# Pairs of feed-forward tiles by block products in stage 1, and 62 modulation steps moved into layer 2

## The chip, the cores and the metric

One core of a Trainium2 chip runs the whole kernel in one launch. The metric is the device time in microseconds (us) of that core, and every time below comes from the chip: from the runs of the kernel before or from one profiled execution of it.

## The reference, cut to what matters

Two hybrid layers (retention, gated linear attention, forgetting attention, then a feed-forward stage) are followed by a second block with two more feed-forward stages, all in float32, for 512 positions and a model width of 1024. What the change touches is the modulation and the feed-forward stage of the two hybrid layers:

```python
def hybrid_layer(x, c_act, ...):                     # called for layer 1, then layer 2
    mod = c_act @ w_ada + b_ada                      # 1024 x 6144, one row of c
    shift1, scale1, gate1, shift2, scale2, gate2 = jnp.split(mod, 6, axis=-1)
    h = modulate(rms_norm(x, norm1_g), shift1, scale1)
    ...                                              # three mixers, out projection
    h2 = modulate(rms_norm(x, norm2_g), shift2, scale2)
    u, g = jnp.split(h2 @ w_up, 2, axis=-1)          # 1024 x 5632
    u = causal_dwconv(u, w_conv, b_conv)             # three taps along the positions
    y = (jax.nn.silu(u) * g) @ w_down                # 2816 x 1024
    return x + (gate2[:, None, :] * y).astype(x.dtype)
```

## The kernel before, in words

**Products.** Activations lie transposed in SBUF, a feature per partition and 512 positions per row. Each float32 product is made of three matmuls on rounded parts (hi x hi, hi x lo, lo x hi; L515 to L517 in `dot`). A tile is 128 outputs: 8 blocks of 128 inputs, three matmuls of 512 columns each. A feed-forward stage has 22 columns f, each with an up tile and a gate tile, and two sweeps of 8 down tiles `d` (after f = 7 and f = 14, 7 blocks of inputs each), with a last sweep of 8 behind f = 21 as `out_proj`. The stages are `ffn(0)` and `ffn(1)` in the two hybrid layers and `ffn(2)`, `ffn(3)` in the second block.

**Pairs.** For an f in `PAIRS_OF[i]` the up and the gate tile are made together by a scheme of seven block products rather than eight (`pair` L1259, on PE `half_product` L1253 to L1255: twelve matmuls of 256 columns each). It needs sums of the weight's blocks (DVE `pair_sums`, L3108, L3111, L3113), their rounded parts (ACT `pair_high`, L2083 and following; DVE `pair_low`, L3122, L3127, L3131, where L3127 is the low part of the pair's second chunk), sums and differences of the activations' halves made once a stage (`halves_whole`, `halves_sum`, `halves_low`, L3046 to L3095, and `halves_high` on ACT), and DVE additions into the results (`pair_out`, L3141, L3146, L3150). The sixth of the seven products adds into a bank that ACT copies first (`pair_copies`, L2102: MP). In ACT's program that copy stands behind `pair_high` of the next pair, and so behind the next pair's sums on DVE. `PAIRS_OF` is empty for stage 0 and holds 10, 14 and 14 columns for the others.

**Behind the tiles.** For each f the DVE makes two convolution taps of the up tile (L3019, L3022), multiplies with the gate tile (L3030) and makes the low part FL (L3036); ACT makes silu and FH. `down_update` adds a down tile to X.

**Weights.** They stream through a ring of six slots (`raw`, `hi`, `lo`; NSLOT = 6), one chunk (512 KB, or 448 KB for a down tile) in each. SP issues the loads in order (L3548 here). The load of chunk n waits until chunk n-6 has been used: by the last matmul of its tile or pair (semaphore `dense_product`), or by DVE where the chunk was a modulation chunk (`dve_norm`). ACT rounds the chunk to hi (L1530), POOL makes lo (L3522) for all but the second chunk of a pair.

**Modulation.** `mod` of a layer is 12 row groups q of 512 outputs, each with four chunks of w_ada (`ada`, L2576). A chunk costs two steps of the generator. In the first DVE does two multiply-adds into AA (L2590 for the very first, L2593), with the fourth chunk also a transpose (L2616) and a reduction (L2620). So a layer has 96 steps and 48 chunks. After some of the q (`ADA_LAST`) PE folds the sums over the partitions, 8 records of 4 matmuls (L801), and DVE adds the result into MOD (L2508). These stand in each engine's program where `schedule` puts them: `beside(main, ada, n)` advances the modulation by one step at each of the first n yields of the main work, `weave(main, fill)` at each, and neither does it at a yield of BUSY. Each engine walks the same schedule, so the order is fixed for all.

**What runs where.** Layer 1's own modulation is made in layer 1 (`beside` with 6, 14, 8 and 22 steps), with its last 14 steps at the head of `ffn(0)`; then all 96 steps of layer 2 run in `ffn(0)` and the `out_proj` behind it. Layer 2 has no modulation work of its own.

Of the kernel before, what the change touches and what calls it, by code (L numbers as in the profile page):

```python
# [33 lines left out]
BUSY = "busy"  # L34
# [8 lines left out]

PAIRS_OF = ((),
# [8 lines left out]
DOWN = {7: (0, 7), 14: (7, 7)}  # L53
LAST = 14


# [73 lines left out]

ADA_LAST = ((6, 9, 11), (3, 7, 11))

# [285 lines left out]
def schedule(P):  # L418

    P.startup()  # L420
    P.prologue()
    P.half_left = False
    for l in range(DEPTH):
        P.layer_begins(l)
        P.order = BIG4
        ada = (y for q in range(4, 12) for y in P.ada(0, q)) if l == 0 else iter(())
        drain(beside(P.ret_inputs(l), ada, 6))
# [16 lines left out]

        def fill_next(l=l, ada=ada):
            yield from ada
            if l + 1 < DEPTH:
                for q in range(12):
                    yield from P.ada(l + 1, q)

# [33 lines left out]
class TensorSteps(Steps):  # L484
# [814 lines left out]
    def down(self, i, wd, k0, kn):  # L1299

        m, t = self.m, self.t
        for d in range(KD):
            key = ("down", i, k0, d)
# [4 lines left out]
                      m.vtake.at("ff", i, k0 + k)) for k in range(kn)]  # L1308
            yield from self.dot(self.bank[b][:, :], terms, [key, ("chunk", n)], (m.lo.at(n), self.free[b]))
            self.free[b] = m.vtake.at(*key)  # L1310
# [202 lines left out]
class ScalarSteps(Steps):  # L1513
# [603 lines left out]
    def ffn(self, i):  # L2117

        def take(j):
            self.ffn_jobs(i, j)  # L2120
            if PAIRS_OF[i] and PAIRS_OF[i][0] < 7 and j == 3:
                self.halves_high(i)
            if PAIRS_OF[i] and PAIRS_OF[i][0] >= 7 and 5 <= j <= 8:
                self.halves_high(i, (j - 5,))
# [3 lines left out]
        for f in range(HEAD, KF):  # L2128
# [22 lines left out]
            if f in DOWN:  # L2151
# [6 lines left out]
                for d in range(KD):  # L2158
                    if g is not None and d >= KD - 2:
                        for part in ((0, 1) if d == KD - 2 else (2,)):  # L2160
                            self.pair_high(i, g, part)
                    yield from self.tile()

# [186 lines left out]
class VectorSteps(Steps):  # L2350
# [704 lines left out]
    def halves_sum(self, i, j):  # L3055
# [12 lines left out]
        else:  # L3068
            q.wait_ge(m.vtake.at("whole", i, 3), m.vtake.at("traw", i, 2))
            e.tensor_tensor(R4, R4, R2, ALU.add).then_inc(*m.vtake.up(("traw", i, 3)))  # L3070

    def halves_step(self, i, j):

        spread = PAIRS_OF[i][0] >= 7
        if spread and 1 <= j <= 4:
# [93 lines left out]
    def ffn(self, i):  # L3169
# [9 lines left out]
        for f in range(HEAD, KF):  # L3179
# [16 lines left out]
            if f in DOWN:  # L3196
# [3 lines left out]
                for d in range(KD):  # L3200
# [3 lines left out]
                    if g is not None and d == KD - 1:  # L3204
                        self.pair_low(i, g, 1)
                        self.pair_low(i, g, 2)
                    yield from self.tile()
                    self.down_update(i, DOWN[f][0], d, gate)
        self.late_tile(i, late, None)

# [597 lines left out]
```

## Time and profile before

| | |
|---|---|
| median of 3 runs | 2869.91 us (2868.97 to 2870.55) |
| profiled execution, its own time | 2871.7 us |
| span of that execution | 2869.9 us |
| TensorE busy | 2830.1 us (99%) |
| VectorE busy | 1744.3 us (61%) |
| ScalarE busy | 1217.9 us (42%) |
| GpSimd busy | 1096.6 us (38%) |
| granted TensorE clock, mean | 0.998 |

TensorE is busy for nearly the whole span, so what counts is how long it works and where it waits. The other engines run beside it with room on average; the room differs from stage to stage. The profiled execution lasted 1.8 us longer than the median, and the span is 1.8 us shorter than that execution's own time.

### The profile page before, as it was taken

To read this page: it belongs to the slowest core of one execution; us is meant where nothing else is said; L and a number is where in the kernel's file an instruction comes from. 1 tells how busy PE (TensorE), PEld (TensorE's weight loads), DVE (VectorE), ACT (ScalarE), POOL (GpSimd) and SP (SyncE) were. 2 spreads that over 40 slices of the span, in tenths; PEclk is the share of its full clock that TensorE was granted. 3 is DMA by queue.
4 is the path that set the end of the run, shared out by engine and by line. 5 is a ranking of instruction groups with operands and counts; after the bars stand their busy time and mean duration, and the time that the engine had idled before them with its cause. 6 is when DMAs were issued, how large, how long until landed. Compare 5 with 4: busy or idle time off the path is not lost.

```text
span 2869.9 us, 38579 instructions
## 1 busy us (share of the span) xinstructions
PE 2830.1 (99%) x16103; PEld 2414.1 (84%) x16103; DVE 1744.3 (61%) x2394; ACT 1217.9 (42%) x1861; POOL 1096.6 (38%) x447
## 2 busy tenths in 40 slices
PE   8999999999999999999999999999999999999999
PEld 5777889888888887789898998889999877789998
DVE  5444598667664624437765855648667556576683
ACT  4335344442333424533443434344334466443433
POOL 1332243444445332342444344543334433333432
PEclk9999999999999999999999999999999999999999
DMA  8431344446564422233333333333333322233332
GB/s 259 126 103 52 96 141 131 118 147 204 188 202 125 117 76 59 74 96 96 89 107 94 100 96 94 104 96 90 109 103 103 96 66 69 75 91 98 110 102 75
DMA packets 507297, 314.32 MB, mean 110 GB/s; under 512 B 14290, under 2 KB 478836, under 8 KB 506868
## 3 DMA queue, kind: packets, MB, share of 16 engines
q1 hardware_dynamic: 507124, 311.87, 37.0%
q8 instruction: 127, 2.08, 0.3%
q14 instruction: 46, 0.38, 0.0%
HBM read 309.73 MB, written 2.10 MB: 109 GB/s over the span
## 4 chain that ended last, share of the span: by engine, by line
PE 92%; DVE 4%; ACT 1%; DMA 1%; SPq 1%; POOL 1%; issue 1%; DVEq 0%; ACTq 0%
PE b L515 14%; PE b L517 14%; PE b L516 14%; PE s L516 3%; PE s L515 3%; PE s L517 3%; PE b L1253 3%; PE o L515 3%; PE b L1255 3%; PE b L1254 3%; PE o L516 3%; PE o L517 3%; PE s L1253 2%; PE s L1255 2%; PE s L1254 2%; PE b L1191 1%
## 5 line engine op out<-in xcount | busy, mean ns | idle before, releaser
L3522 POOL TENSOR_TENSOR lo<-raw,hi 128x1024 fp32r<-128x1024 f32 (+3 forms) x437 | 1094.3, 2514 | 1744.1 <-ACT hi L1530 1258.2
L1530 ACT ACTIVATE hi<-raw 128x1024 fp32r<-128x1024 f32 (+1 forms) x440 | 449.6, 1034 | 300.7 <-DMA raw<-in_w_up_dram 93.3
L515 PE MATMUL b<-HH,hi 128*128 128x512 f32 x1080 | 433.4, 401 | 1.6 <-DVE X L2419 1.6
L517 PE MATMUL b<-HH,lo 128*128 128x512 f32 x1080 | 421.2, 390 | 0.0
L516 PE MATMUL b<-HL,hi 128*128 128x512 f32 x1080 | 421.1, 390 | 0.0
L515 PEld LDWEIGHTS b<-HH,hi 128*128 128x128 f32 x1080 | 202.8, 188 | 51.7 <-issue 7.1
L517 PEld LDWEIGHTS b<-HH,lo 128*128 128x128 f32 x1080 | 202.7, 188 | 43.5
L516 PEld LDWEIGHTS b<-HL,hi 128*128 128x128 f32 x1080 | 203.0, 188 | 41.7 <-issue 1.4
L515 PE MATMUL b<-FH,hi 128*128 128x512 f32 (+1 forms) x391 | 144.8, 370 | 1.5 <-POOL lo L3522 1.5
L516 PE MATMUL b<-FL,hi 128*128 128x512 f32 (+1 forms) x391 | 144.5, 370 | 0.0
L517 PE MATMUL b<-FH,lo 128*128 128x512 f32 (+1 forms) x391 | 144.5, 369 | 0.0
L2593 DVE SCALAR_TENSOR_TENSOR AA<-raw,CA,AA 128x512 f32<-128x512 f32 x140 | 139.0, 993 | 3.0
L3036 DVE TENSOR_TENSOR FL<-CB,FH 128x512 fp32r<-128x512 f32 x88 | 84.9, 964 | 64.8 <-ACT FH L2058 64.8
L2083 ACT ACTIVATE EH<-ER 128x1024 fp32r<-128x1024 f32 x38 | 40.3, 1061 | 181.5 <-DVE ER L3108 181.5
L3127 DVE TENSOR_TENSOR lo<-raw,hi 128x1024 fp32r<-128x1024 f32 x52 | 109.2, 2100 | 0.0
L2051 ACT ACTIVATE CB<-CB 128x512 f32<-128x512 f32 x88 | 55.4, 630 | 122.3 <-DVE CB L3022 72.0
L2058 ACT ACTIVATE FH<-CB 128x512 fp32r<-128x512 f32 x88 | 55.6, 631 | 119.4 <-DVE CB L3030 118.3
L515 PE MATMUL s<-HH,hi 128*128 128x512 f32 x232 | 90.3, 389 | 0.0
L516 PE MATMUL s<-HL,hi 128*128 128x512 f32 x232 | 90.3, 389 | 0.0
L517 PE MATMUL s<-HH,lo 128*128 128x512 f32 x232 | 90.2, 389 | 0.0
L515 PEld LDWEIGHTS b<-FH,hi 128*128 128x128 f32 x391 | 73.7, 189 | 14.3 <-POOL lo L3522 1.9
L517 PEld LDWEIGHTS b<-FH,lo 128*128 128x128 f32 x391 | 73.7, 189 | 12.5
(765 smaller groups left out, 7485.6 us busy)
## 6 DMA issues: line engine op xcount, KB each, us to landing
raw<-in_w_up_dram SPq DMA_DIRECT2D x88, 512.0 KB, 4.1
raw<-in_w_ada_dram SPq DMA_DIRECT2D x80, 512.0 KB, 4.9
raw<-in_w_in_dram SPq DMA_DIRECT2D x76, 512.0 KB, 4.0
raw<-in_w_mg_dram SPq DMA_DIRECT2D x48, 512.0 KB, 3.8
raw<-in_ffn_w_gate_dram SPq DMA_DIRECT2D x44, 512.0 KB, 3.8
raw<-in_ffn_w_up_dram SPq DMA_DIRECT2D x44, 512.0 KB, 3.9
raw<-in_w_down_dram SPq DMA_DIRECT2D x32, 448.0 KB, 3.8
raw<-in_ffn_w_down_dram SPq DMA_DIRECT2D x32, 448.0 KB, 4.1
```

The lines of the kernel that those rows point to most:

```text
L515: e.matmul(out, wh, xh, start=start and k == 0, stop=False)
L516: e.matmul(out, wh, xl, start=False, stop=False)
L517: mm = e.matmul(out, wl, xh, start=False, stop=stop and k == last)
L1253: e.matmul(out, wh[:, c], xh[:, k, :], start=start and k == 0, stop=False, skip_group_check=True)
L1254: e.matmul(out, wh[:, c], xl[:, k, :], start=False, stop=False, skip_group_check=True)
L1255: mm = e.matmul(out, wl[:, c], xh[:, k, :], start=False, stop=k == 3, skip_group_check=True)
L1530: e.activation(t["hi"][:, c % NSLOT, 0:w], K.raw[:, c % NSLOT, 0:w], ACT.Copy).then_inc(*m.hi.up(c))
L2058: e.activation(t["FH"][:, f % ROOM, :], t["CB"][:, f % 2, :], ACT.Copy).then_inc(*m.atake.up(("fh", i, f)))
L2593: a = e.scalar_tensor_tensor(out=AA[:, :], in0=raw[:, k * 512:k * 512 + 512], scalar=CA[:, kk:kk + 1], in1=AA[:, :], op0=ALU.mult, op1=ALU ...
L3036: e.tensor_tensor(t["FL"][:, f % ROOM, :], t["CB"][:, f % 2, :], t["FH"][:, f % ROOM, :].bitcast(F32), ALU.subtract).then_inc(*m.vtake.up( ...
L3127: e.tensor_tensor(t["lo"][:, s, :], K.raw[:, s, :], t["hi"][:, s, :].bitcast(F32), ALU.subtract).then_inc(*m.vtake.up(("lo", na + 1 if K.p ...
L3522: e.tensor_tensor(t["lo"][:, s, 0:w], K.raw[:, s, 0:w], t["hi"][:, s, 0:w].bitcast(F32), ALU.subtract).then_inc(*m.lo.up(n))
```

## The change

`PAIRS_OF[0]` becomes (8, 9, 10, 12, 13, 15, 16, 17, 19, 20): ten columns of `ffn(0)` are made as pairs, and f = 4 to 7, 11, 14, 18 and 21 stay direct. The halves of the activations that pairs need are made beside the first down sweep (`halves_beside_down`, ACT's `halves_high` at d = 2 and 3), where no modulation step is taken any more (`rows_beside`). `pair` itself yields BUSY as before, so a pair takes no step either. Layer 2's 96 steps are now one generator `rows` that goes on across the layers: up to 34 of them in `ffn(0)`, behind layer 1's last 14 (48 in all), then 6 + 14 + 8 + 22 = 50 in layer 2's own stages, and the last 12 at the head of `ffn(1)`. `ADA_LAST[1]` gets a fourth fold: (3, 6, 9, 11).

```diff
--- before.py
+++ after.py
@@ -1,5 +1,5 @@
 from contextlib import ExitStack
-from itertools import chain
+from itertools import chain, islice
 
 import concourse.bass as bass
 import numpy as np
@@ -41,7 +41,7 @@
 
 
 
-PAIRS_OF = ((),
+PAIRS_OF = ((8, 9, 10, 12, 13, 15, 16, 17, 19, 20),
             (7, 8, 9, 11, 12, 14, 15, 16, 18, 19),
             (5, 6, 7, 8, 9, 10, 12, 13, 14, 15, 16, 17, 19, 20),
             (5, 6, 7, 8, 9, 10, 12, 13, 14, 15, 16, 17, 19, 20),
@@ -52,6 +52,9 @@
 ROOM = 8
 DOWN = {7: (0, 7), 14: (7, 7)}
 LAST = 14
+def rows_beside(i, f, d):
+    return i > 0 or (f == LAST and d < 7)
+
 
 
 def ffn_next(i, f):
@@ -128,7 +131,7 @@
 
 
 
-ADA_LAST = ((6, 9, 11), (3, 7, 11))
+ADA_LAST = ((6, 9, 11), (3, 6, 9, 11))
 
 
 def ada_group(l, q_):
@@ -420,10 +423,11 @@
     P.startup()
     P.prologue()
     P.half_left = False
+    rows = (y for q in range(12) for y in P.ada(1, q))
     for l in range(DEPTH):
         P.layer_begins(l)
         P.order = BIG4
-        ada = (y for q in range(4, 12) for y in P.ada(0, q)) if l == 0 else iter(())
+        ada = (y for q in range(4, 12) for y in P.ada(0, q)) if l == 0 else rows
         drain(beside(P.ret_inputs(l), ada, 6))
         drain(P.ret_values(l))
         P.order = ["b0", "b1"]
@@ -442,11 +446,10 @@
         P.mods(l, 1)
         drain(P.out_proj("w_o", l, P.x_norm(2 * l + 1)))
 
-        def fill_next(l=l, ada=ada):
+        def fill_next(l=l, ada=ada, rows=rows):
             yield from ada
             if l + 1 < DEPTH:
-                for q in range(12):
-                    yield from P.ada(l + 1, q)
+                yield from islice(rows, 34)
 
         fill = fill_next()
         weave(P.ffn(l), fill, False)
@@ -1306,7 +1309,8 @@
             hi, lo = self.K.slot(n, kn, 128)
             terms = [(hi[:, k, :], lo[:, k, :], t["FH"][:, (k0 + k) % ROOM, :], t["FL"][:, (k0 + k) % ROOM, :],
                       m.vtake.at("ff", i, k0 + k)) for k in range(kn)]
-            yield from self.dot(self.bank[b][:, :], terms, [key, ("chunk", n)], (m.lo.at(n), self.free[b]))
+            for _ in self.dot(self.bank[b][:, :], terms, [key, ("chunk", n)], (m.lo.at(n), self.free[b])):
+                yield None if rows_beside(i, k0 + kn, d) else BUSY
             self.free[b] = m.vtake.at(*key)
 
 
@@ -2118,9 +2122,9 @@
 
         def take(j):
             self.ffn_jobs(i, j)
-            if PAIRS_OF[i] and PAIRS_OF[i][0] < 7 and j == 3:
+            if i > 1 and j == 3:
                 self.halves_high(i)
-            if PAIRS_OF[i] and PAIRS_OF[i][0] >= 7 and 5 <= j <= 8:
+            if i == 1 and 5 <= j <= 8:
                 self.halves_high(i, (j - 5,))
 
         yield from self.projects(range(2 * HEAD), ffn_norm(i), take)
@@ -2159,7 +2163,10 @@
                     if g is not None and d >= KD - 2:
                         for part in ((0, 1) if d == KD - 2 else (2,)):
                             self.pair_high(i, g, part)
-                    yield from self.tile()
+                    for _ in self.tile():
+                        yield None if rows_beside(i, f, d) else BUSY
+                    if i == 0 and f == 7 and d in (2, 3):
+                        self.halves_high(i, (2 * d - 4, 2 * d - 3))
 
 
 
@@ -3069,9 +3076,21 @@
             q.wait_ge(m.vtake.at("whole", i, 3), m.vtake.at("traw", i, 2))
             e.tensor_tensor(R4, R4, R2, ALU.add).then_inc(*m.vtake.up(("traw", i, 3)))
 
+    def halves_beside_down(self, i, d):
+
+        if d < 2:
+            self.halves_whole(i, (2 * d, 2 * d + 1))
+        elif d < 4:
+            self.halves_sum(i, 2 * d - 4)
+            self.halves_sum(i, 2 * d - 3)
+        elif d < 6:
+            self.halves_low(i, (2 * d - 8, 2 * d - 7))
+
     def halves_step(self, i, j):
 
-        spread = PAIRS_OF[i][0] >= 7
+        spread = i == 1
+        if i == 0:
+            return
         if spread and 1 <= j <= 4:
             self.halves_whole(i, (j - 1,))
         elif spread and 5 <= j <= 8:
@@ -3204,8 +3223,11 @@
                     if g is not None and d == KD - 1:
                         self.pair_low(i, g, 1)
                         self.pair_low(i, g, 2)
-                    yield from self.tile()
+                    for _ in self.tile():
+                        yield None if rows_beside(i, f, d) else BUSY
                     self.down_update(i, DOWN[f][0], d, gate)
+                    if i == 0 and f == 7:
+                        self.halves_beside_down(i, d)
         self.late_tile(i, late, None)
 
     def down_update(self, i, k0, d, gate):
```

On SP, the loads behind the first down sweep of `ffn(0)`. Before, every tile's chunk is followed by a modulation chunk, here at the end of the sweep:

```order
152 L3548 DMA raw<-in_w_down_dram 128x7x128 [waits dense_product]
153 L3548 DMA raw<-in_w_ada_dram 128x2x512 [waits dve_norm]
154 L3548 DMA raw<-in_w_up_dram 128x8x128 [waits dense_product]
155 L3548 DMA raw<-in_w_ada_dram 128x2x512 [waits dve_norm]
156 L3548 DMA raw<-in_w_up_dram 128x8x128 [waits dense_product]
```

Now the seven w_up chunks at the top end with 11's up tile; a w_ada chunk, 11's gate tile and another w_ada chunk follow, and then both chunks of pair 12, those of pair 13, and the two tiles of f = 14 with the down sweep:

```order
145 L3570 DMA raw<-in_w_up_dram 128x8x128 [waits dense_product] x7
146 L3570 DMA raw<-in_w_ada_dram 128x2x512
147 L3570 DMA raw<-in_w_up_dram 128x8x128 [waits dense_product]
148 L3570 DMA raw<-in_w_ada_dram 128x2x512
149 L3570 DMA raw<-in_w_up_dram 128x8x128 [waits dense_product]
150 L3570 DMA raw<-in_w_up_dram 128x8x128
151 L3570 DMA raw<-in_w_up_dram 128x8x128 [waits dense_product]
152 L3570 DMA raw<-in_w_up_dram 128x8x128 [waits dve_norm]
153 L3570 DMA raw<-in_w_up_dram 128x8x128 [waits dense_product]
154 L3570 DMA raw<-in_w_ada_dram 128x2x512 [waits dve_norm]
```

What moved: between the chunks of pair 10 and those of pair 12 there are now four others, two direct tiles and two modulation chunks, so that the slots that pair 12's chunks go into are pair 10's. The same holds at f = 18 for pairs 17 and 19.

On DVE, around f = 18 of `ffn(0)`. Before, with modulation steps between direct tiles only:

```order
604 L3036 TENSOR_TENSOR FL<-CB,FH 128x512
605 L2593 SCALAR_TENSOR_TENSOR AA<-raw,CA,AA 128x512 x2
606 L3019 SCALAR_TENSOR_TENSOR CB<-b,PAR,CB 128x511
607 L3022 SCALAR_TENSOR_TENSOR CB<-b,PAR,CB 128x510
608 L2593 SCALAR_TENSOR_TENSOR AA<-raw,CA,AA 128x512 x2
609 L2616 STREAM_TRANSPOSE raw<-AA 128x512
610 L2620 TENSOR_REDUCE AS<-raw 128x16
611 L3030 TENSOR_TENSOR CB<-CB,b 128x512
612 L3036 TENSOR_TENSOR FL<-CB,FH 128x512
```

Now, behind the low parts of pair 19's sums (L3150), the two multiply-adds, transpose and reduction of a row group's last chunk, then the convolution of f = 18:

```order
651 L3150 TENSOR_TENSOR EL<-ER,EH 128x512
652 L2600 SCALAR_TENSOR_TENSOR AA<-raw,CA,AA 128x512 x2
653 L2623 STREAM_TRANSPOSE raw<-AA 128x512
654 L2627 TENSOR_REDUCE AS<-raw 128x16
655 L3026 SCALAR_TENSOR_TENSOR CB<-o,PAR,CB 128x511
656 L3029 SCALAR_TENSOR_TENSOR CB<-o,PAR,CB 128x510
657 L2597 TENSOR_SCALAR AA<-raw,CA 128x512
658 L2600 SCALAR_TENSOR_TENSOR AA<-raw,CA,AA 128x512
659 L2515 TENSOR_TENSOR MOD<-s,PAR 128x16
660 L3037 TENSOR_TENSOR CB<-CB,s 128x512
661 L3043 TENSOR_TENSOR FL<-CB,FH 128x512
662 L3127 TENSOR_TENSOR ER<-raw 128x1024
```

What moved: the reduction (L2627) that the fold on PE waits for stands behind pair 19's sums and low parts, and pair 20's sums (L3127) behind all of it.

On DVE, at f = 5 of `ffn(1)`. Before, only the low parts of the halves (L3095) stand between the tiles' rows:

```order
1074 L3030 TENSOR_TENSOR CB<-CB,b 128x512
1075 L3036 TENSOR_TENSOR FL<-CB,FH 128x512
1076 L3095 TENSOR_TENSOR TL<-TR,TH 128x1024
1077 L3019 SCALAR_TENSOR_TENSOR CB<-o,PAR,CB 128x511
1078 L3022 SCALAR_TENSOR_TENSOR CB<-o,PAR,CB 128x510
1079 L3095 TENSOR_TENSOR TL<-TR,TH 128x1024
1080 L3030 TENSOR_TENSOR CB<-CB,s 128x512
```

Now layer 2's last modulation chunks stand between them as well, with the fold's result added into MOD (L2515):

```order
1171 L3043 TENSOR_TENSOR FL<-CB,FH 128x512
1172 L3114 TENSOR_TENSOR TL<-TR,TH 128x1024
1173 L2600 SCALAR_TENSOR_TENSOR AA<-raw,CA,AA 128x512 x2
1174 L2623 STREAM_TRANSPOSE raw<-AA 128x512
1175 L2627 TENSOR_REDUCE AS<-raw 128x16
1176 L3026 SCALAR_TENSOR_TENSOR CB<-b,PAR,CB 128x511
1177 L3029 SCALAR_TENSOR_TENSOR CB<-b,PAR,CB 128x510
1178 L3114 TENSOR_TENSOR TL<-TR,TH 128x1024
1179 L2515 TENSOR_TENSOR MOD<-o,PAR 128x8
```

What moved: two multiply-adds, a transpose and a reduction have come between FL (L3043) and the next convolution (L3026). On PE the fold of these sums stands in the middle of 5's gate tile.

## Rows read from the trace of the kernel before

**Rows 1.** The page: the chain that ended last, by engine.

```profile
PE 92%; DVE 4%; ACT 1%; DMA 1%; SPq 1%; POOL 1%; issue 1%; DVEq 0%; ACTq 0%
```

**Rows 2.** Timeline of PE, `ffn(2)`: start, duration, operation, [idle before, releaser].

```profile
2044.16 0.28 PE L1253 MATMUL b<-HH,hi 128*128 128x256 f32 x1
...
2074.39 0.40 PE L515 MATMUL s<-HH,hi 128*128 128x512 f32 x1
...
2085.30 0.28 PE L1253 MATMUL b<-HH,hi 128*128 128x256 f32 x1
```

**Rows 3.** Waits of PE, window 908 to 914: total, times, longest, in us.

```profile
PE b L515 <- POOL lo L3522: 1.5, 1, 1.5
```

**Rows 4.** Timeline of PE around a fold, at the end of `ffn(0)`.

```profile
916.80 0.39 PE L517 MATMUL b<-FH,lo 128*128 128x512 f32 x1
...
917.31 0.39 PE L515 MATMUL o<-FH,hi 128*128 128x256 f32 x1
```

**Rows 5.** DMA view, window 2054 to 2062: KB, us from issue to landing.

```profile
raw<-in_ffn_w_gate_dram SPq DMA_DIRECT2D x1, 512.0 KB, 4.0
raw<-in_ffn_w_up_dram SPq DMA_DIRECT2D x1, 512.0 KB, 5.3
```

**Rows 6.** Timeline of DVE in `ffn(1)`, between two groups of pairs.

```profile
1610.69 1.21 DVE L3108 TENSOR_TENSOR ER<-raw 128x1024 f32<-128x1024 f32 x1
...
1616.92 1.21 DVE L3127 TENSOR_TENSOR lo<-raw,hi 128x1024 fp32r<-128x1024 f32 x1
...
1620.04 0.68 DVE L3131 TENSOR_TENSOR EL<-ER,EH 128x512 fp32r<-128x512 f32 x1
1621.05 0.75 DVE L3019 SCALAR_TENSOR_TENSOR CB<-b,PAR,CB 128x511 f32<-128x511 f32 x1 [0.32 <-ACT CB L2044]
...
1623.35 0.69 DVE L3030 TENSOR_TENSOR CB<-CB,b 128x512 f32<-128x512 f32 x1 [0.77 <-ACT CB L2051]
...
1625.34 1.22 DVE L3108 TENSOR_TENSOR ER<-raw 128x1024 f32<-128x1024 f32 x1
```

**Rows 7.** Timeline of PE there: the sixth product of a pair.

```profile
1629.65 0.38 PE L1253 MATMUL o<-TH,hi 128*128 128x256 f32 x1 [0.79 <-ACT MP L2102]
```

**Rows 8.** Timeline of DVE in `ffn(0)`: a modulation row's end.

```profile
611.82 1.53 DVE L2593 SCALAR_TENSOR_TENSOR AA<-raw,CA,AA 128x512 f32<-128x512 f32 x2
...
615.00 0.69 DVE L3030 TENSOR_TENSOR CB<-CB,b 128x512 f32<-128x512 f32 x1 [0.18 <-PE b L517]
...
617.67 0.47 DVE L2590 TENSOR_SCALAR AA<-raw,CA 128x512 f32<-128x512 f32 x1
618.18 0.75 DVE L2593 SCALAR_TENSOR_TENSOR AA<-raw,CA,AA 128x512 f32<-128x512 f32 x1
```

**Rows 9.** Timeline of DVE in the first down sweep of `ffn(1)`.

```profile
1595.23 3.43 DVE L3127 TENSOR_TENSOR lo<-raw,hi 128x1024 fp32r<-128x1024 f32 x1
```

**Rows 10.** Timeline of POOL at the same time.

```profile
1594.13 3.45 POOL L3522 TENSOR_TENSOR lo<-raw,hi 128x1024 fp32r<-128x1024 f32 x1 [6.08 <-DVE ER L3113]
```

**Rows 11.** Timeline of PE: marks of the mixers of layers 1 and 2.

```profile
105.28 0.59 PE L844 MATMUL s<-rq,rk 128*128 128x512 f32 x1
...
561.06 0.36 PE L654 MATMUL t<-ones,SQ 128*128 128x1 f32 x2
...
1003.18 0.59 PE L844 MATMUL s<-rq,rk 128*128 128x512 f32 x1
...
1455.89 0.25 PE L654 MATMUL t<-ones,SQ 128*128 128x1 f32 x1
```

**Rows 12.** Waits of PE, window 80 to 90 (layer 1's `ret_values`).

```profile
PE b L515 <- POOL lo L3522: 1.1, 1, 1.1
```

**Rows 13.** Timeline of PE in `ffn(1)`: the gate tile of f = 5 begins.

```profile
1525.95 0.39 PE L515 MATMUL s<-HH,hi 128*128 128x512 f32 x1
```

**Rows 14.** Timeline of DVE in the same place.

```profile
1527.35 1.21 DVE L3095 TENSOR_TENSOR TL<-TR,TH 128x1024 fp32r<-128x1024 f32 x1
```

**Rows 15.** The page's costliest groups: count, busy us, mean ns.

```profile
L2593 DVE SCALAR_TENSOR_TENSOR AA<-raw,CA,AA 128x512 f32<-128x512 f32 x140 | 139.0, 993 | 3.0
```

## The prediction

> **What bounds the kernel now.** I began with the chain that ended last: 92% of the span lies on PE [rows 1], and PE is busy for 99% of it by the table above. The change can therefore gain only by giving PE less to do or by ending a wait of PE, and it loses wherever PE is made to wait. So the next views were PE's timeline, its waits stage by stage, and, where the changed order puts new work between what PE waits for, the timelines of DVE and POOL and the DMA view. The sum is made against the profiled execution's own 2871.7 us, of which the span is 2869.9; the median of the runs is 2869.91, 1.8 lower, and the forecast is brought to it at the end.
>
> **What it takes away.** Stage 2 already runs the same pairs. Three pairs take 2074.39 - 2044.16 = 30.23 us, 10.08 each, and the two direct tiles behind them 10.91 [rows 2]. A pair is 84 matmuls of 256 columns instead of 48 of 512, and gives 0.83 us. Ten: **-8.3**. At the head of layer 1's out projection PE waits once for POOL's lo, 1.5 us [rows 3]: POOL is behind there because modulation chunks, which free their slots late, stand between all tiles. They are gone from the end of stage 0: **-1.5**. A fold holds PE up by 917.31 - 916.80 less one matmul's 0.23, some 0.3 [rows 4]; two leave the stage: **-0.6**. Together -10.4.
>
> **Pair 12, by the ring.** What is new is when pair 12's weights arrive. Its two chunks take the slots of pair 10's, and these come free only when pair 10 ends. Count from the start of pair 8. Pair 10 ends at 30.24, the two tiles of f = 11 end at 41.15, and pair 12's sixth product, five products of 1.44 in, is wanted at 48.35. SP issues the loads at about 30.4. Two loads that were issued together landed after 4.0 and 5.3 us [rows 5], so DVE's sums of pair 12 begin at 36.1 instead of 30.3. From there I follow DVE. Between two groups of pairs, from one pair's sums to the next pair's, it took 1625.34 - 1610.69 = 14.65 [rows 6]. The new order has one modulation chunk more there, 0.5 + 0.75 and 1.53 us [rows 8], of which 0.32 + 0.77 falls into time in which DVE waited for ACT [rows 6]: 16.35. The copy that the sixth product waits for stands on ACT behind the next pair's high parts, and that product began 1629.65 - 1625.34 = 4.3 after the next pair's sums [rows 6, 7]. So pair 12's sixth product begins at 36.1 + 16.35 + 4.3 = 56.75: **+8.4**. Bounds: with the loads in time the same chain gives 30.3 + 16.35 + 4.3 = 50.95, +2.6; and if POOL stands in DVE's way once (3.43 for a low part that takes 1.21 elsewhere [rows 6, 9]), +10.6.
>
> **f = 18 and pair 19.** The ring is late in the same way. Here a row group also ends: DVE makes pair 19's sums and low parts (1620.04 + 0.68 - 1610.69 = 10.0 [rows 6]) and behind them two multiply-adds, transpose and reduction, 615.00 - 611.82 = 3.1 [rows 8]. PE's fold is due at 41.15 and gets its sums at 36.1 + 10.0 + 3.1 = 49.2: **+8.0**, or +2.3 with the loads in time. Then DVE needs 5.0 to pair 20's sums (convolution 1.5, modulation 1.25, gate and FL 1.4, the rest waiting for ACT), so the sixth product of pair 19 comes at 49.2 + 5.0 + 4.3 = 58.5, where PE is ready at 56.8: **+1.7**.
>
> **Pair 15 and the first down sweep.** Pair 15's second chunk lies in the slot of a down tile that ends only three tiles before the pair, and POOL takes 3.45 us where DVE works against it [rows 10]. From nothing to the 2.2 by which such a low part is longer: half, **+1.1**. In the first down sweep DVE now makes the halves beside eight shorter tiles and POOL makes lo beside it; nothing of this was there. At least nothing; at most two such collisions, 4.4; since DVE has no modulation there any more I take **+1.5**.
>
> A rule bears on this. DVE's low part of 3.43 us began 1.1 after a POOL instruction of 3.45 and the same operation takes 1.21 elsewhere [rows 6, 9, 10]. The Trainium skill, page "SBUF — State Buffer", section "Who interferes with whom", says that a DVE instruction with two inputs in SBUF and a GpSimd instruction that reads SBUF exclude each other, the later one blocked fully rather than slowed. By that rule the trace agrees for this low part, but the modulation's multiply-add also has two inputs in SBUF and is 0.99 us on average against 0.75 alone [rows 8, 15]. Full blocking at every new meeting would bring the sum nearer to the worse of the rivals below.
>
> Another rule is about the load. The rows show 4.0 and 5.3 us [rows 5]. The Trainium skill, page "DMA: Bandwidth & Descriptors", section "Anatomy of one DMA — SWDGE (gpsimd) path", gives 2.0 us and bytes / 436e3 for a transfer of another kind of queue, an estimate of 3.2 us for one of these. By it each of the two ring terms would be some 2 us smaller, and the total 4 us; I keep to the rows.
>
> **Layer 2.** Its 50 steps have the same places as layer 1's. From the first scores to the last sums of the mixers layer 1 took 561.06 - 105.28 = 455.78 and layer 2, without modulation, 1455.89 - 1003.18 = 452.71 [rows 11]: 3.1 with two folds in it. In `ret_values`, before the first mark, layer 1 waited 1.1 for POOL [rows 12]. **+4.2**. It could be 0.6, the folds alone, if those differences have other causes.
>
> **Stage 1's head.** Twelve steps end in a fold, 0.3, which stands in the middle of 5's gate tile, due at 1525.95 + 2.7 = 1528.7 [rows 13]. Before it DVE has the low part that ends at 1527.35 + 1.21 = 1528.5 [rows 14] and then 3.1 for multiply-adds, transpose and reduction [rows 8]: 1531.6, 2.9 late. **+3.2**; from 0.3, if DVE is early, to 5.5 if it meets POOL.
>
> **The sum.** -10.4 + 8.4 + 8.0 + 1.7 + 1.1 + 1.5 + 4.2 + 3.2 = +17.7. 2871.7 + 17.7 = 2889.4, less 1.8: **2887.6 us**.
>
> **Rivals.** *The loads are no worse than DVE's order.* If the pairs' chunks are in SBUF when DVE gets to them, the two ring terms are 2.6 and 2.3: 11.5 less, 2876.1. For it: no pair of the trace waited for a load. Against it: the changed order on SP, which names pair 10's slots. *More collisions.* The 50 steps in layer 2 and the halves in the sweep meet POOL, and each multiply-add grows by 0.99 - 0.75 = 0.24 [rows 8, 15]; 100 of them are 24 us of DVE, and if four tenths of it lie where PE waits for DVE, 10 more: 2897.6. *Faster.* DVE catches up: it is busy for only 61%, and if the sums of pairs 12 and 19 reach ACT when they do in stage 2, the sixth product waits 0.8 twice [rows 7], as there. Then the sum is -8.3 - 1.5 - 0.6, three folds or 0.9 in later stages and 1.6 of waits, -7.9: 2862.0. It decides at the start of pair 12's sums: this rival is right if they begin by 48.35 + 0.8 - 4.3 - 16.35 = 28.5, before pair 10 ends. The slots speak against it; only a DVE that runs well ahead of PE, or an ACT copy that doesn't have to wait, would make it so. That the change doesn't do what it says is ruled out by the order of the instructions.
>
> **How the numbers follow.** The forecast gets 0.57, loads in time 0.18, more collisions 0.14, faster 0.11. What a measurement of this kernel can tell from no change is about 0.2%, 5.7 us. Faster by more than that: 0.09, most of the last rival. Slower by more: the forecast and the collisions whole and most of the second case, which lies 6.2 above the median, with some 0.09 of it within: 0.80. Within: 0.11. The range leaves out the faster rival and the upper end of the collisions, and takes in the bounds of the two ring terms, 2873 to 2898.
>
> **What would show it.** In the profile of the changed kernel: pairs of 10.08 us in stage 0; PE waiting at L1253 for ACT's MP some 8 us in pair 12; PE waiting at the fold some 8 us at f = 18, and again some 2 in pair 19; a wait of 3 at the fold in `ffn(1)`; the mixers of layer 2 as long as layer 1's, 455.8; no wait at the head of the first out projection. The prediction is wrong if the sums of pair 12 begin with pair 10's end, if loads land in under 3 us, or if PE's waits in stage 0 come to under 8 us in all.

## The result and the profile after

The changed kernel takes **2896.36 us** (median of 4 runs, 2895.70 to 2896.57) against 2870.23 us before (4 runs): 1.0089 of it, 95% interval 1.0077 to 1.0101. It is slower by 26.1 us, where 17.7 were forecast (2887.6); the time lies within the range of 2873 to 2898, near its upper end. The profiled execution took 2895.7 us, with a span of 2893.9, 24.0 more than the profiled span before.

The page of the changed kernel, engines' busy time and the chain by engine, beside [rows 1]:

```profile
PE 2827.7 (98%) x16471; PEld 2427.3 (84%) x16471; DVE 1857.4 (64%) x2497; ACT 1242.5 (43%) x1905; POOL 1082.4 (37%) x437
...
PE 88%; DVE 6%; ACT 2%; DMA 1%; issue 1%; POOL 1%; SPq 1%; DVEq 0%; ACTq 0%
```

PE is busy for 2.4 us less than before although the span is 24.0 longer: the pairs do save work, and part of that is lost again to slow stretches, which count as busy. Part of the chain has moved from PE (92% before) to DVE (4%, now 6%) and ACT (1%, now 2%).

Waits of PE over the whole span (total, times, longest); line numbers are 3 to 22 higher than before, the letter is the bank that PE writes, so L804 is the fold (L801), L1256 a block product (L1253), L3544 POOL's lo and L2106 ACT's copy:

```profile
PE s L804 <- DVE AS L2627: 10.2, 1, 10.2
PE b L1256 <- POOL lo L3544: 7.7, 2, 6.8
...
PE o L804 <- DVE AS L2627: 5.8, 1, 5.8
...
PE b L1256 <- ACT MP L2106: 1.9, 2, 1.1
...
PE o L1256 <- ACT MP L2106: 1.4, 1, 1.4
```

None of the first three was there before. They are the fold in front of pair 19, pair 12's first product (6.8 of the 7.7; the rest is pair 15's), and the fold in `ffn(1)`. PE's timeline places them; the last row is the start of pair 8 in `ffn(2)`, as the first of [rows 2]:

```profile
559.97 0.36 PE L657 MATMUL t<-ones,SQ 128*128 128x1 f32 x2
...
695.71 0.31 PE L1256 MATMUL o<-HH,hi 128*128 128x256 f32 x1
...
725.96 0.40 PE L518 MATMUL b<-HH,hi 128*128 128x512 f32 x1
...
743.86 0.58 PE L1256 MATMUL b<-HH,hi 128*128 128x256 f32 x1 [6.82 <-POOL lo L3544]
...
753.98 0.38 PE L1256 MATMUL o<-TH,hi 128*128 128x256 f32 x1 [1.44 <-ACT MP L2106]
...
870.03 0.31 PE L804 MATMUL s<-AS,CON 128*32 128x16 f32 x8 [10.16 <-DVE AS L2627]
870.27 0.58 PE L1256 MATMUL b<-HH,hi 128*128 128x256 f32 x1
...
880.24 0.28 PE L1256 MATMUL b<-TH,hi 128*128 128x256 f32 x1
...
931.30 0.28 PE L518 MATMUL o<-FH,hi 128*128 128x256 f32 x1
...
1018.25 0.59 PE L847 MATMUL s<-rq,rk 128*128 128x512 f32 x1
...
1473.15 0.25 PE L657 MATMUL t<-ones,SQ 128*128 128x1 f32 x1
...
1552.78 0.30 PE L804 MATMUL o<-AS,CON 128*32 128x8 f32 x8 [5.84 <-DVE AS L2627]
...
2071.64 0.28 PE L1256 MATMUL b<-HH,hi 128*128 128x256 f32 x1
```

Pairs 8 to 10 take 725.96 - 695.71 = 30.25 us, as in [rows 2]. Layer 2's mixers take 1473.15 - 1018.25 = 454.90, against 452.71 in [rows 11]. The same places of PE's program in both profiles tell where the 24.0 us of the spans arose (the 10.3 is all of the forecast's terms but those of layer 2 and `ffn(1)`):

| stretch | from the rows | longer by | forecast |
|---|---|---|---|
| up to layer 1's last sums | 559.97 - 561.06 | -1.1 | 0 |
| stage 0 and the head of the out projection | 931.30 - 917.31 = 13.99, and 1.09 | 15.1 | 10.3 |
| to layer 2's last sums | 1473.15 - 1455.89 = 17.26, less 13.99 | 3.3 | 4.2 |
| `ffn(1)`, and on to pair 8 of `ffn(2)` | 2071.64 - 2044.16 = 27.48, less 17.26 | 10.2 | 3.2 |
| the rest of the second block | 24.0 less 27.48 | -3.5 | 0 |

SP issues pair 12's loads when pair 10 has ended, at 726.16:

```profile
726.16 20.21 SPq L3570 DMA_DIRECT2D raw<-in_w_up_dram  x5
```

DVE in the two places of stage 0, and at the head of `ffn(1)`:

```profile
724.73 0.69 DVE L3160 TENSOR_TENSOR MP<-MP,s 128x512 f32<-128x512 f32 x1 [1.10 <-PE s L1258]
...
732.03 1.23 DVE L3127 TENSOR_TENSOR ER<-raw 128x1024 f32<-128x1024 f32 x1 [5.89 <-DMA raw<-in_w_up_dram]
...
741.52 2.56 DVE L2597 TENSOR_SCALAR AA<-raw,CA 128x512 f32<-128x512 f32 x1
...
746.24 1.53 DVE L2600 SCALAR_TENSOR_TENSOR AA<-raw,CA,AA 128x512 f32<-128x512 f32 x2
...
749.67 1.22 DVE L3127 TENSOR_TENSOR ER<-raw 128x1024 f32<-128x1024 f32 x1
...
864.89 3.62 DVE L2600 SCALAR_TENSOR_TENSOR AA<-raw,CA,AA 128x512 f32<-128x512 f32 x2
...
869.29 0.69 DVE L2627 TENSOR_REDUCE AS<-raw 128x16 f32<-128x512 f32 x1
...
1544.30 3.42 DVE L3114 TENSOR_TENSOR TL<-TR,TH 128x1024 fp32r<-128x1024 f32 x1
1547.65 3.61 DVE L2600 SCALAR_TENSOR_TENSOR AA<-raw,CA,AA 128x512 f32<-128x512 f32 x2
```

POOL at the same times (the last row is three low parts):

```profile
723.93 2.41 POOL L3544 TENSOR_TENSOR lo<-raw,hi 128x1024 fp32r<-128x1024 f32 x1 [4.59 <-ACT hi L1534]
...
741.30 2.50 POOL L3544 TENSOR_TENSOR lo<-raw,hi 128x1024 fp32r<-128x1024 f32 x1 [14.96 <-ACT hi L1534]
...
864.67 2.50 POOL L3544 TENSOR_TENSOR lo<-raw,hi 128x1024 fp32r<-128x1024 f32 x1 [14.92 <-ACT hi L1534]
...
1541.41 8.51 POOL L3544 TENSOR_TENSOR lo<-raw,hi 128x1024 fp32r<-128x1024 f32 x3 [3.20 <-ACT hi L1534]
```

DVE waits 5.89 us for the load that the prediction speaks of. The rows at 741.52, 864.89, 1544.30 and 1547.65 begin inside one of POOL's low parts, and each is some 2 us longer than its like elsewhere. Not every row is: the addition at 724.73, which has one of its inputs in PSUM, began 0.8 into a low part of 2.41 and took 0.69, as elsewhere.

ACT in pair 12, and the copy (MP) that pair 19's sixth product needs:

```profile
739.65 0.63 ACT L2062 ACTIVATE FH<-CB 128x512 fp32r<-128x512 f32 x1 [2.23 <-DVE CB L3037]
740.19 1.04 ACT L1534 ACTIVATE hi<-raw 128x1024 fp32r<-128x1024 f32 x1
...
878.26 0.58 ACT L2106 ACTIVATE MP<-b 128x512 f32<-128x512 f32 x1
```

Stretches behind the waits and one inside a wait, 860 to 870 (window and its length, busy time of PE, PEld, DVE, ACT, POOL, granted clock, DMA share, GB/s). Behind 6.8, 10.2 and 5.8 us of idle time the clock is down, and before the fold at 870.03 it is down while PE still waits; in the stretch with the wait of 1.4 it is not:

```profile
744.00:750.00 6.00, 6.00 (x41) 6.00 (x42) 5.20 (x9) 2.21 (x3) 0.00 (x0) 0.78 0.69 194
750.00:756.00 6.00, 4.56 (x39) 4.36 (x37) 5.83 (x5) 4.23 (x6) 3.51 (x2) 1.00 0.19 70
...
860.00:870.00 10.00, 0.00 (x0) 0.00 (x0) 9.20 (x11) 2.87 (x4) 2.50 (x1) 0.64 0.00 0
870.00:880.00 10.00, 9.97 (x67) 9.94 (x67) 9.06 (x12) 6.23 (x9) 2.61 (x1) 0.68 0.60 157
...
1552.00:1560.00 8.00, 7.22 (x26) 5.76 (x27) 4.08 (x8) 1.26 (x2) 0.00 (x0) 0.57 0.22 65
```

A clock of 0.78 over 6 us is 1.3 us of full-speed time lost, 0.68 over 10 is 3.2 and 0.57 over 8 is 3.4, at most: up to 8.0 us for which the prediction has no term. Not all of it made the kernel longer, as the last part shows.

### The profile page after: what moved, and what is told of

Read it like the earlier page. It is cut to its first block, busy times and chain, and to the rows that moved or that the text cites. A ratio compares the mean times of both kernels' runs of the same rounds, so it can differ in the third digit from the quotient of the medians.

```text
span 2893.9 us, 39467 instructions
## 1 busy us (share of the span) xinstructions
PE 2827.7 (98%) x16471; PEld 2427.3 (84%) x16471; DVE 1857.4 (64%) x2497; ACT 1242.5 (43%) x1905; POOL 1082.4 (37%) x437
## 4 chain that ended last, share of the span: by engine, by line
PE 88%; DVE 6%; ACT 2%; DMA 1%; issue 1%; POOL 1%; SPq 1%; DVEq 0%; ACTq 0%
PE b L518 13%; PE b L520 12%; PE b L519 12%; PE b L1256 4%; PE b L1258 4%; PE b L1257 4%; PE s L518 3%; PE s L519 3%; PE s L520 3%; PE o L518 3%; PE o L519 3%; PE o L520 3%; PE s L1256 2%; PE s L1258 2%; PE s L1257 2%; PE b L1194 1%
## 5 line engine op out<-in xcount | busy, mean ns | idle before, releaser
L3544 POOL TENSOR_TENSOR lo<-raw,hi 128x1024 fp32r<-128x1024 f32 (+2 forms) x427 | 1080.1, 2540 | 1782.3 <-ACT hi L1534 1248.7
L1534 ACT ACTIVATE hi<-raw 128x1024 fp32r<-128x1024 f32 (+2 forms) x430 | 438.6, 1033 | 262.4 <-DMA raw<-in_w_in_dram 59.9
L518 PE MATMUL b<-HH,hi 128*128 128x512 f32 x1016 | 410.2, 404 | 0.3 <-POOL lo L3544 0.3
L519 PE MATMUL b<-HL,hi 128*128 128x512 f32 x1016 | 397.3, 391 | 0.0
L520 PE MATMUL b<-HH,lo 128*128 128x512 f32 x1016 | 397.2, 391 | 0.0
L3146 DVE TENSOR_TENSOR lo<-raw,hi 128x1024 fp32r<-128x1024 f32 x62 | 129.5, 2089 | 0.0
L3043 DVE TENSOR_TENSOR FL<-CB,FH 128x512 fp32r<-128x512 f32 x88 | 75.1, 853 | 62.4 <-ACT FH L2062 62.4
L518 PE MATMUL b<-hi,HH 128*128 128x512 f32 (+1 forms) x208 | 81.2, 390 | 3.6 <-POOL lo L3544 3.6
L1256 PE MATMUL b<-HH,hi 128*128 128x256 f32 x256 | 74.1, 289 | 7.7 <-POOL lo L3544 7.7
L3141 DVE TENSOR_TENSOR EL<-ER,EH 128x1024 fp32r<-128x1024 f32 x48 | 76.6, 1596 | 3.0
L520 PE MATMUL b<-hi,HL 128*128 128x512 f32 (+1 forms) x208 | 77.9, 374 | 0.0
```

Of the source, the lines that this page charges most:

```text
L518: e.matmul(out, wh, xh, start=start and k == 0, stop=False)
L519: e.matmul(out, wh, xl, start=False, stop=False)
L520: mm = e.matmul(out, wl, xh, start=False, stop=stop and k == last)
L1256: e.matmul(out, wh[:, c], xh[:, k, :], start=start and k == 0, stop=False, skip_group_check=True)
L1534: e.activation(t["hi"][:, c % NSLOT, 0:w], K.raw[:, c % NSLOT, 0:w], ACT.Copy).then_inc(*m.hi.up(c))
L3043: e.tensor_tensor(t["FL"][:, f % ROOM, :], t["CB"][:, f % 2, :], t["FH"][:, f % ROOM, :].bitcast(F32), ALU.subtract).then_inc(*m.vtake.up( ...
```

## The experiments

Theory: pair 12 and pair 19 wait because their chunks lie in the slots of the pair just before; the folds wait for rows that stand behind late sums. Main rival: DVE has too much to do between pairs. Times are medians; before is 2870.43 to 2871.12 in their four sets. In the diffs `QUIET` is a set of (f, tile) of stage 0 that yield BUSY in all engines (the diffs show only the lines that matter, and one that stands in several engines' programs is shown once):

```diff
-                        yield BUSY if f == KF - 1 else None
+                        yield None if tile_beside(i, f, u) else BUSY      # False for QUIET
```

**No steps at f = 11 and 18, eight steps in the first sweep.**

```diff
+QUIET = {(11, 0), (11, 1), (18, 0), (18, 1)}
-    return i > 0 or (f == LAST and d < 7)
+    return i > 0 or (f == LAST and d < 7) or (f == 7 and d < 4)
```

> The changed kernel, but f = 11 and f = 18 of ffn(0) take no modulation step; the eight steps (four chunks) stand beside down tiles 0 to 3 of the first down sweep instead. Nothing is left out. Ring theory: pair 12's chunks then take the slots of pair 9's, which come free one pair earlier, DVE's sums of pair 12 begin as pair 10 ends (30.3 us from the start of pair 8, not 36.3), and of the waits of pair 12 (7.0 and 1.6) and at f = 18 (10.3), with 1.3 and 2.8 lost in the half-clock stretches behind them, at most 0.8 each is left: 21 us less, 0 to 3 more in the first down sweep, so about 2877. Rival (it is not the loads but DVE that has too much to do near the pairs): the same here, so this run only sizes what both claim; the next one tells them apart. Second rival (the stalls come from elsewhere, pairs cost too much DVE in stage 0 anyway): the waits stay above 4 us each, over 2885.

Measured: 2884.69, 1.0048 (1.0033 to 1.0063), 7.7 above the 2877. Waits of PE, window 695 to 770, and POOL's low part at the first of them:

```profile
PE o L1263 <- POOL lo L3551: 5.3, 1, 5.3
PE o L1263 <- ACT MP L2113: 0.8, 1, 0.8
```

```profile
697.67 3.40 POOL L3551 TENSOR_TENSOR lo<-raw,hi 128x1024 fp32r<-128x1024 f32 x1 [9.67 <-DVE ER L3139]
```

The second row is all that is left of pair 12's waits, and pair 19 has 0.8. The first is new: pair 8 waits for POOL's low part, which waited for DVE's sums, and DVE has the modulation chunks of the sweep before them. So the stalls of pair 12 and of the fold come from the steps at f = 11 and 18. The run took away their chunks and DVE's rows together and can't tell which of the two it was. The new place takes back about half of what that gives.

**Steps at the up tiles only.**

```diff
+QUIET = {(11, 1), (18, 1)}
+    return i > 0 or (f == LAST and d < 7) or (f == 7 and d < 2)
```

> The changed kernel, but only the up tiles of f = 11 and f = 18 take modulation steps; the other four steps stand beside down tiles 0 and 1 of the first sweep. Nothing is left out. Half of DVE's extra rows between the pairs is gone, but the second chunk of pair 12 still takes a slot of pair 10's. Ring theory: DVE's sums of pair 12 still begin 36.3 us after pair 8's start, the waits of pair 12 and of pair 19 together stay at 6 to 8 us each, and only the fold's wait at f = 18 and what its clock cost goes, since the fold now stands behind a reduction made in the down sweep: 2888 to 2893. Rival (DVE's amount of work sets the stall): the waits go by half, to 4 us each, and the time to about 2883.

Measured: 2894.98, 1.0086. Waits of PE, window 695 to 770, and then 810 to 900:

```profile
PE o L1263 <- ACT MP L2113: 5.9, 1, 5.9
...
PE b L1263 <- ACT MP L2113: 8.7, 2, 6.1
```

Half of the rows are gone from DVE, but the two pairs still wait 5.9 and 6.1 us. That is at the low end of the ring theory's 6 to 8 and above the rival's 4. DVE still waits for pair 12's load, though 3.96 us and not 5.89, so the sums begin earlier than the expectation has them:

```profile
732.32 1.23 DVE L3134 TENSOR_TENSOR ER<-raw 128x1024 f32<-128x1024 f32 x1 [3.96 <-DMA raw<-in_w_up_dram]
```

With one modulation chunk less in between, only the second of pair 12's chunks takes a slot of pair 10's. The time is 2 above its range: pair 8 and pair 15 wait longer here (1.6 and 2.6).

**The move alone, no pairs in stage 0.**

```diff
+    rows = (y for q in range(12) for y in P.ada(1, q))      # in before
-        ada = (y for q in range(4, 12) for y in P.ada(0, q)) if l == 0 else iter(())
+        ada = (y for q in range(4, 12) for y in P.ada(0, q)) if l == 0 else rows
-ADA_LAST = ((6, 9, 11), (3, 7, 11))
+ADA_LAST = ((6, 9, 11), (3, 6, 9, 11))
-                for q in range(12):
-                    yield from P.ada(l + 1, q)
+                yield from islice(rows, 34)
```

> The kernel before with the move of layer 2's modulation alone (34 steps at most in ffn(0) behind the 14, 50 in layer 2, 12 in ffn(1), four folds), and no pairs in stage 0. Nothing is left out. If the parts add up as they do in the profile: -2.1 at the first out projection, +3.4 in layer 2, +10 at the head of ffn(1) (6.0 at the fold, 3.2 of half clock behind it, the rest folds and tails): 2881.5, 1.0039 of before. Rival (the 10 us come from the state in which the pairs leave the engines): ffn(1) loses 3 as forecast, 2875.

Measured: 2880.14, 1.0031 (1.0020 to 1.0043), 9.3 above before. In window 1490 to 1560:

```profile
PE s L801 <- DVE AS L2620: 5.9, 1, 5.9
```

The fold's wait in `ffn(1)` is that of the changed kernel to 0.1: it has nothing to do with stage 0's pairs. The move alone costs 9.3 (2881.5 was expected), and the pairs with their stalls add the rest of the 26.1.

**Layer 2's last twelve steps in its mixing** (`beside(P.mixing(l, range(2, 12)), ada, 34 if l else 22)`).

> The changed kernel with layer 2's last twelve steps in its mixing (34 steps instead of 22) and none in ffn(1). Nothing is left out. Theory: the 6.0 us wait at the fold, the slow stretch behind it (3.2) and the rest of the 10 go, and the mixing, where pairs take no step either, pays 0 to 1: 2887. Rival (the modulation's rows collide with POOL wherever they stand): layer 2 takes back 4 or more, 2891 or above.

Measured: 2895.69, 1.0088. The mixing yields only 22 free steps, so no instruction moved and this is the changed kernel a second time. It tests nothing but the repetition: 0.7 from the first.

**The eight steps beside layer 1's gla inputs.**

```diff
+QUIET = {(11, 0), (11, 1), (18, 0), (18, 1)}
-        fill = P.gla_inputs(l)
+        fill = beside(P.gla_inputs(l), ada, 0 if l else 8)
```

> The changed kernel with no modulation step at f = 11 and f = 18 of ffn(0), as in quiet_11_18, but the eight steps stand beside the gla inputs of layer 1, where DVE is busy under half of the time, and the first down sweep stays as the changed kernel has it. Nothing is left out. The run before had pair 12 and pair 19 down to waits of 1.0 and lost 5.4 us in front of pair 8, to POOL's low part behind the modulation chunks in the sweep. Theory: those 5.4 and the clock they cost are gone too, the move costs 0 to 1 in layer 1, and 22 us go in all: 2874, 1.0015 of before. Rival (the halves made in the first sweep hold up pair 8 whatever stands beside it): at least 3 us of wait remain in front of pair 8, 2878 or more.

Measured: 2890.76, 1.0071. Waits in window 700 to 900, the whole of stage 0's pairs, are 0.8 and 1.7 for ACT's copy and 0.5 for POOL; pair 8 has none, so the halves don't hold it up. But in window 200 to 290:

```profile
PE t L998 <- DVE foxP L2809: 6.3, 4, 4.2
PE o L978 <- ACT foxC L1854: 5.2, 1, 5.2
```

The forgetting attention needs DVE in time, though DVE is busy there for under half (22.8 us of the 50 from 200 on, before). The changed kernel waits 1.5 and 0.7 there. The run is 17 above the expectation and shows that busy share is no measure of room.

**The last fold two tiles later.**

```diff
         if q_ == 11:
+            for _ in range(4 if l else 0):      # four more yields for the other engines too
+                yield None
             self.ada_last()
```

> The changed kernel, with the last fold of layer 2's modulation (on PE, and its addition on DVE) four steps later, behind two more tiles of ffn(1); all modulation rows on DVE stay where they are. Nothing is left out. Theory: the wait of 6.0 and the slow stretch behind it (3.2) come from the place of the fold on PE alone, so 9 us go: 2887. Rival (DVE and POOL are behind at the head of ffn(1), and PE will wait for them at the next tile or pair instead): 5 us or more of the wait reappear by the first down tile, 2893 or above.

Measured: 2893.31, 1.0079. The fold no longer waits, and in window 1500 to 1580 stands instead

```profile
PE b L1258 <- POOL lo L3550: 3.7, 1, 3.7
```

in front of the stage's first pair. 3 us are won, not 9: the rival was right in kind (its 5 us of wait are 3.7), DVE and POOL are behind there. This and the version before it together:

> quiet_b and fold_later together. Nothing is left out. If the two add up, 31 us go: 2865, 0.998 of before, which is faster than both. Rival (each leaves something the other hid, or the 3.3 us by which the second block ended earlier in the profile of the changed kernel were chance): 2868 to 2872, no different from before.

Measured: 2890.03, 1.0066, where 2865 was expected and 2868 to 2872 by the rival: both missed. It is 0.7 under the run with the gla inputs alone and 3.3 under the one with the later fold alone, so the gla inputs keep what they cost, and most of the 3 us of the later fold is not seen again. Why is open.

**Three chunks per column at f = 4 to 7**, instead of steps at f = 11 and 18 (two more `yield None` behind each up tile).

> The changed kernel with no modulation step at f = 11 and f = 18 of ffn(0); the eight steps follow the up tiles of f = 4 to 7, where each f then takes six instead of four. Nothing is left out. The two earlier versions showed the waits of pairs 12 and 19 gone (1.0 each) and paid for the steps' new place (5.4 in front of pair 8, 16 beside the gla inputs). Theory: direct tiles have room for three chunks in two tiles, so nothing new is paid and 22 us go: 2874, 1.001 of before. Rival (POOL or DVE falls behind with three chunks in two tiles): waits of 3 us or more at f = 5 to 8, 2878 or above.

Measured: 2889.72, 1.0067. Window 590 to 700:

```profile
PE b L811 <- DVE AS L2640: 5.8, 1, 5.8
PE b L525 <- POOL lo L3560: 4.5, 1, 4.5
```

The rival held: with three chunks in two tiles a fold waits as in `ffn(1)`, and the last tile before the sweep waits for POOL. Pairs 12 and 19 wait at most 0.9, as in the other runs without these steps.

**Twelve more steps in the first out projection** (`islice(rows, 46)`).

> The changed kernel with 46 instead of 34 of layer 2's steps before layer 2: the twelve more stand beside layer 1's last out projection, and ffn(1) has none. Nothing is left out. Theory: all that ffn(1)'s head lost goes (6.0 at the fold, 3.2 of half clock behind it, 0.5), and the out projection takes back the 1.5 of POOL and a fold that it had before: 2888. Rival (DVE and POOL are behind there too): the out projection loses 5 or more, 2892 or above.

Measured: 2903.54, 1.0116. `ffn(1)` waits no more, and in window 920 to 975 PE waits at layer 2's first three tiles (L569), right behind the out projection:

```profile
PE b L569 <- POOL lo L3544: 6.2, 2, 4.5
PE o L569 <- POOL lo L3544: 1.8, 1, 1.8
```

This and the version before it together:

> early_11_18 and rows_out_proj together. Nothing is left out. If they add up: 22 and 8 less, 2866, 0.9985 of before, faster than both by a little over what can be told. Rival (one of the new places costs what the other run shows by itself): 2870 or more.

Measured: 2895.62, 1.0086. The sum of the two would be 2896.9. In both cases the rival held. Four places were tried for steps (the first sweep, the gla inputs, f = 4 to 7, the out projection), and each took back about half or more of what their leaving was expected to give.

**Fewer pairs.** Then the count was turned round: as many pairs as leave room for the steps where they cost nothing.

```diff
-PAIRS_OF = ((8, 9, 10, 12, 13, 15, 16, 17, 19, 20),
+PAIRS_OF = ((8, 9, 10, 15, 16, 17),
-                yield from islice(rows, 34)
+                yield from islice(rows, 46)
```

> The changed kernel with six pairs in stage 0, f = 8, 9, 10 and 15, 16, 17, and 46 instead of 34 of layer 2's steps in ffn(0): the four columns that are direct again have room for sixteen steps, so ffn(1) has none, and no pair stands behind a direct column with steps. Nothing is left out. If the parts found so far add up: six pairs -5.0, out projection -2.1 with one fold more in the stage +0.3, layer 2 +3.4, pair 15's two waits +2.4, nothing at f = 12, 18 and in ffn(1): -1.0, no different from before, 2870. Rival (a load or a modulation row near pairs 8 or 15 costs what it cost in front of pair 8 in quiet_11_18): 5 more, 2875.

Measured: 2869.81 (11 runs), 0.9997 of before (0.9988 to 1.0006). The waits in window 690 to 900; the first two are pair 15's, and no other pair of stage 0 waits:

```profile
PE b L1256 <- ACT MP L2106: 1.1, 1, 1.1
PE s L1256 <- POOL lo L3544: 1.0, 1, 1.0
PE o L1194 <- DVE CB L3037: 0.2, 1, 0.2
```

And with `f == LAST and d < 5` in `rows_beside`:

> six_pairs with no step beside down tiles 5 and 6 of the second sweep (four steps fewer, taken up by f = 20), so that the chunks in front of pair 15 get their slots a modulation chunk earlier. Nothing is left out. Theory: pair 15's waits (1.1 for POOL, 1.3 for ACT's copy) fall to the 0.9 of the other pairs, 1.5 less than six_pairs: 2868.5, the fastest of all, if by less than can be told. Rival (those waits are DVE's and POOL's collisions and stay): as six_pairs.

Measured: 2869.43 (11 runs), 0.9992 (0.9983 to 1.0001). The first two rows are gone altogether. Against the before of the same set, 2871.12, it is 1.7 us less: the lowest median of all, and not told from no change. Both came out within 1 us of the sum of the parts. That fits the parts but is no sharp test of them, since the sum is near nothing and "no change" would have fitted too.

## Why the prediction was right, and where its sum was short

- **The saving.** Forecast -8.3 for ten pairs and -2.1 at the out projection. Three pairs take 30.25, and no wait is left at the head of the out projection.
- **Pair 12, by the ring: the cause right, the place half seen.** DVE's sums begin 732.03 - 695.71 = 36.3 after pair 8's start (forecast 36.1), the next sums 749.67 - 732.03 = 17.6 later (16.35; the extra is the 2.56 us row), and the sixth product 4.3 after them. PE waits 6.8 + 1.4 = 8.2, forecast 8.4, but that the two agree is partly luck: the sixth product begins 753.98 - 695.71 = 58.3 after pair 8, 9.9 later than the 48.35 at which it is wanted, and what is not wait is slow clock. The size that was missed is DVE's lengthened row. SP's row at 726.16, the wait of 5.89 and the two runs at f = 11 and 18 show that the loads' slots are the cause. What I had not seen is that most of the wait is at the first product and not at the sixth: ACT's rounding of the pair's first chunk (740.19) stands behind FH (739.65), which waits for DVE, and POOL's low part behind that.
- **f = 18: mechanism right, size short.** 10.2 for 8.0. The step that failed is 3.1 us for the row group's end: the two multiply-adds took 3.62 instead of 1.53, since POOL was at work. The forecast 1.7 of pair 19 was not there, because the slow clock hid it: the copy it needs was ready at 878.26 + 0.58 = 878.84, PE came at 880.24, and at full speed it would have come at 870.27 + 5 x 1.44 = 877.47 and waited 1.4.
- **Pair 15: undersized.** 0.9 + 1.1 for 1.1. **First sweep: oversized.** No wait in front of pair 8, for 1.5.
- **Layer 2: about right.** 3.3 for 4.2: 2.2 in the mixers, and before them a wait of 0.9 for POOL in `ret_values`.
- **`ffn(1)`: the term most in error.** Forecast 3.2; the stretch is 10.2 longer, and the wait alone is 5.8. Before the reduction DVE had two rows of 3.42 and 3.61 us that take 1.21 and 1.53 without POOL, 4.3 us more. This was the upper bound that I named (5.5, if it meets POOL), and I took the value without a meeting. Most of the remaining 4.4 is the slow clock behind it, up to 3.4.
- **Missing: the clock.** The prediction priced waits as waits. Behind the three long ones PE runs at the lower of its two levels for some microseconds, up to 8.0 us in all. That is close to the 8.4 by which the sum was short, but it is not the explanation of it. In pair 12 the slow stretch, up to 1.3, cost nothing of its own: ACT's copy for the sixth product stands behind DVE's sums and came as long after them as in [rows 6, 7] (4.3), and a faster PE would have waited for it longer. In pair 19 five products took 880.24 - 870.27 = 9.97 and not 7.2, 2.8 more, of which 1.4 would have been a wait. Only behind the fold in `ffn(1)` does all of it count. Some 5 us are left for the clock (1.4 + 3.4), worked out from the rows and tested by no run of its own. The other misses are DVE's rows that met POOL: 1.3, 2.1 and 2.6.
- **Why the time lies in the range: partly luck.** The three stretches that the prediction has terms for came to 15.1 + 3.3 + 10.2 = 28.6, 10.9 over the 17.7; added to 2869.9 that is 2898.5, just beyond the range. In the two profiles -1.1 and -3.5 came in where nothing was changed.
- **A row that was missed.** The profile before had a slow stretch too, 0.83 in the ten microseconds around a wait of 1.9 for DVE, and I did not read it:

```profile
2460.00:2470.00 10.00, 8.11 (x37) 6.49 (x35) 9.03 (x11) 3.75 (x6) 0.00 (x0) 0.83 0.00 0
```

That row lies in the second block, where nothing was changed. In the profiled execution after, the same wait has a clock of 1.00, and in the changed kernel's second run (the one with 22 free steps) 0.83 again: the same instructions, so this is chance. A wait of 1.6 for DVE's X, which the page of before shows, is missing as well. It is missing in every trace but that of before, so it may be that one execution's or the kernel's, and with one trace of the kernel before that stays open. Together they are most of the 3.5 of the table, and a reason not to take the 24.0 of the spans for the 26.1 of the medians.

- **The rivals.** The faster one is out: the sums would have had to begin before pair 10's end. They began 36.3 after pair 8's start, and pair 10 ended at 30.25. Loads in time is out by the 5.89. More collisions was half right: DVE did meet POOL where PE waits for it, in stage 0 and `ffn(1)`, and layer 2 paid little.

On the exclusion of DVE and POOL: the multiply-adds at 864.89 began 0.2 us into a POOL row of 2.50, and lasted 2.1 longer than elsewhere; the first multiplication at 741.52 began 0.2 into another and lasted 2.1 longer. The rest of POOL's row was 2.3 in both cases. The Trainium skill, "SBUF — State Buffer", section "Who interferes with whom", says that the later one is blocked for the whole of the earlier, and for the multiply-add, which has two inputs in SBUF, the trace agrees. The multiplication at 741.52 has one SBUF tensor and a scalar column; by the same section it contends only in a two-port mode, and no run here shows in which mode it ran.

## What to carry to other kernels

When a change makes one stage cheaper by moving work out of it, price the places that the work goes to first: here ten pairs saved some 8.3 us, the 62 displaced steps cost 9.3 even without pairs, and beside ten pairs they cost more wherever they were put; six pairs, with the steps left where they were free, came out even. Count, for each load, whose slot it takes with the new chunks in between, and price a wait of several microseconds on TensorE with the slow stretch behind it, unless another wait follows that it only fills. Of unknown collisions on a chain that ends in a wait of PE, take the bound with the collision.

## What the hardware showed that I had not expected

- A wait of 1.4 us left the granted clock at 1.00 in the stretch around it, and one of 1.9, with shorter ones of 1.0 and 0.7 before it, did so in one execution and not in another of the same kernel (0.83); behind 5.8, 6.8 and 10.2 us of idle PE it was 0.57, 0.78 and 0.68 over 8, 6 and 10 us. Before the fold it had fallen while PE still stood idle (0.64 in 860 to 870).
- A slow stretch can cost less than it takes: where PE would have waited for another engine anyway, in pair 12 and in part in pair 19, it filled the wait.
- DVE at under half busy had no room beside the forgetting attention: four chunks brought PE's waits there to 6.3 and 5.2 us from 1.5 and 0.7.
- A DVE row with its tensor inputs in SBUF that began within one of POOL's low parts was longer by nearly what was left of it, 2.1 of 2.3 us, a multiplication with one tensor input and a scalar column too. Rows with an input in PSUM were not (724.73, 0.69 us).
